# Expert tiles of 96 + 32 slots with one scatter each, and a last token tile routed in halves

## The reference

```
p_g = softmax(h2 @ w_rg + b_rg)                 # 4 groups
g_idx = argmax p_g                              # one group per token
le_sel = logits of the 4 experts of that group
pe_top, e_idx = top_k(softmax(le_sel), 2)       # two experts, both of that group
wts = p_g[g_idx] * pe_top / sum(pe_top)
x = x + sum over the two experts of  wts * (silu(h2 @ w_gate[e]) * (h2 @ w_up[e])) @ w_down[e]
```

## Time and profile before

| | |
|---|---|
| time, median of 3 runs | 559.99 us (556.28 to 560.72) |
| the profiled execution | 559.87 us, span 558.0 us |
| busy in the span | PE 499.4 us (89%), DVE 230.0 (41%), POOL 165.6 (30%), ACT 113.8 (20%) |
| granted TensorE clock, mean | 0.93 |
| scatters that add into `out` (L585) | 25 |

### The profile page before, as it was taken

The page is one execution under the profiler, slowest core; times in us unless marked ns, Lnnn a source line. Parts: engine busy times, 40 slices in busy tenths (PEclk is TensorE's granted clock), DMA queues, the critical chain, the costliest instruction groups (busy, mean ns, idle before and its releaser), DMA issues. The chain is left out here.

```text
span 558.0 us, 7597 instructions
## 1 busy us (share of the span) xinstructions
PE 499.4 (89%) x2858; PEld 267.9 (48%) x2858; DVE 230.0 (41%) x642; ACT 113.8 (20%) x273; POOL 165.6 (30%) x167
## 2 busy tenths in 40 slices
PE   5898899998998999999999997854999999999970
PEld 3554444444664777665666666553333333333320
DVE  1127444412678834444545555452522322223110
ACT  2200242223232243332222311130011000110010
POOL 1211288850789700000000002221035222222242
PEclk9999799998998999999999977665999999999995
DMA  8999500005100000066000229386589999999712
GB/s 290 427 384 404 231 1 1 1 1 194 50 2 0 1 1 0 2 260 267 1 0 1 75 81 374 150 321 234 169 324 342 400 377 388 378 375 380 226 25 32
DMA packets 29609, 100.04 MB, mean 179 GB/s; under 512 B 5376, under 2 KB 6912, under 8 KB 29184
## 3 DMA queue, kind: packets, MB, share of 16 engines
q1 hardware_dynamic: 21216, 84.03, 39.1%
q0 software_dynamic: 5904, 8.43, 6.3%
q10 hardware_dynamic: 2448, 7.04, 3.3%
HBM read 77.39 MB, written 35.21 MB: 202 GB/s over the span
## 5 line engine op out<-in xcount | busy, mean ns | idle before, releaser
L1217 PE MATMUL bank<-arena 128*128 128x512 f32 (+1 forms) x256 | 114.9, 587 | 5.5 <-DVE arena L826 3.1
L1467 PE MATMUL bank<-arena 128*32 128x512 f32 x832 | 93.1, 599 | 0.0
L1192 PE MATMUL bank<-arena 128*128 128x128 f32 (+1 forms) x412 | 61.9, 287 | 21.0 <-DVE arena L908 4.6
L1217 PEld LDWEIGHTS bank<-arena 128*128 128x128 f32 x256 | 49.6, 196 | 61.4 <-issue 54.7
L1192 PEld LDWEIGHTS bank<-arena 128*128 128x128 f32 (+1 forms) x412 | 50.9, 145 | 57.9 <-issue 44.6
L585 POOL DMA_INDIRECT out<-arena x25 | 38.7, 1549 | 122.6 <-DVE arena L1143 49.6
L1355 PE MATMUL bank<-arena 128*128 128x512 f32 x128 | 65.0, 637 | 0.0
L1467 PEld LDWEIGHTS bank<-arena 128*32 128x32 f32 x832 | 25.8, 111 | 57.9 <-issue 57.9
L908 DVE COPY arena<-bank 128x512 f32<-128x512 f32 (+2 forms) x64 | 36.4, 587 | 36.4 <-PE bank L1192 36.3
L467 POOL TENSOR_SCALAR small<-small 128x1 f32<-128x1 f32 x16 | 3.7, 233 | 157.6 <-ACT arena L680 97.1
L1487 PE MATMUL bank<-arena 128*32 128x512 f32 x416 | 47.0, 592 | 0.8 <-DVE arena L1136 0.8
(11 more groups left out here) (153 smaller groups left out, 517.0 us busy)
## 6 DMA issues: line engine op xcount, KB each, us to landing
arena<-in_w_gu SPq DMA_DIRECT2D x17, 2048.0 KB
arena<-in_w_dn SPq DMA_DIRECT2D x17, 1024.0 KB, 20.6
slot_rows<-arena SPq DMA_DIRECT2D x1, 11308.0 KB, 37.8
arena<-slot_rows ACTq DMA_DIRECT2D x13, 514.0 KB, 6.7
arena<-in_w_out SPq DMA_DIRECT2D x2, 2048.0 KB, 8.0
arena<-in_x SPq DMA_DIRECT2D x4, 512.0 KB, 10.7
arena<-in_w_in_k SPq DMA_DIRECT2D x1, 2048.0 KB, 16.3
arena<-in_w_in_q SPq DMA_DIRECT2D x1, 2048.0 KB, 22.3
```

Source lines behind the costliest of these rows:

```text
L1192: last = nc.tensor.transpose(TPB[p % 2][0:s.shape[-1], b * P:(b + 1) * P], s, ident)
L1217: last = nc.tensor.matmul(product_bank(i)[:, 0:width], hT[:, k, t * P:(t + 1) * P], w[:, k, :], start=(k == 0), stop=(k == KD - 1))
L1467: last = nc.tensor.matmul(GU[g % 2][BLK * b:BLK * (b + 1), :], xT[g % 2][:, k, BLK * b:BLK * (b + 1)], w_gu[n % RING][:, k, :], start=(k = ...
```

## The change

It does four things. (1) Tile 3i + j (j = 0, 1, 2) holds the 96 slots of one expert of group i and 32 of the 96 slots of the last expert of group (i + 2) % 4, so no token is in a tile twice. Each tile is added by one scatter, which waits for that of the tile before; 13 scatters take the place of 25. Since own and shared slots lie apart in `slot_rows`, a tile is loaded by two DMAs, of 96 and of 32 rows. (2) Weights are loaded in the order in which tiles need them (`LOADED`), and `buffers()` picks for each load the buffer that is free first. Loads 5 to 16 are issued behind the same tiles as before. (3) `logits_out` finds the two experts by adding -1e30 to the logits of all other groups and taking the top of all 16, in place of cutting out four logits and adding the group's base afterwards. (4) The last token tile is routed in halves: PE and DVE do half b = 0 of its transposes and router products while half b = 1 of the output projection runs; the products of `ranks(3)` with the all-ones matrix are done before the choice is known, in bank 5.

```diff
+TRIPLES = [[EPG * i + j for j in range(3)] + [EPG * ((i + 2) % G) + 3] for i in range(G)]
+LOADED = [TRIPLES[i][j] for i in range(G) for j in (0, 3, 1, 2)]
...
         def loads_of(g):
-            return [(4 * g + b) // 3 if g < ITEMS else E + g - ITEMS for b in range(4)]
+            i, j = divmod(g, 3)
+            return 3 * [4 * i + (0, 2, 3)[j]] + [4 * i + 1] if g < ITEMS else 4 * [E + g - ITEMS]
+        def rows_of(g):
+            if g >= ITEMS:
+                return x_dram[g * P:g * P + CAP, :], x_dram[g * P + CAP:(g + 1) * P, :]
+            i, j = divmod(g, 3)
+            own, shared = CAP * TRIPLES[i][j], CAP * TRIPLES[i][3] + BLK * j
+            return x_dram[own:own + CAP, :], x_dram[shared:shared + BLK, :]
...
-            def add(g, run):
+            def add(g):
                 pool.wait_ge(s_ya, g + 1)
                 pool.wait_ge(s_yv, g + 1)
                 pool.wait_ge(s_tag, g + 1)
+                if g > 0:
+                    pool.wait_ge(s_add[(g - 1) % 3], adds(g - 1))
                 nc.gpsimd.indirect_dma_start(
-                    out=out_rows, out_offset=bass.IndirectOffsetOnAxis(ap=tag_row[:, g, run:run + 1], axis=0),
+                    out=out_rows, out_offset=bass.IndirectOffsetOnAxis(ap=tag_row[:, g, 0:1], axis=0),
...
-                added(g, 0)
-                add(g, 1)
-                add(g + 1, 0)
...
-            added(LAST - 1, 1)
-            add(LAST, 0)
+            for g in range(LAST + 1):
+                add(g)
+                if g < 2:
+                    overflow(2 * g)
+                    overflow(2 * g + 1)
...
-                nc.scalar.dma_start(xg[g % 3], x_dram[g * P:(g + 1) * P, :]).then_inc(s_xg[g % 3], 16)
+                for part, src in ((slice(0, CAP), rows_of(g)[0]), (slice(CAP, P), rows_of(g)[1])):
+                    nc.scalar.dma_start(xg[g % 3][part, :], src).then_inc(s_xg[g % 3], 16)
...
-                link(nc.vector.tensor_scalar(oh, konst[:, K_E:K_E + G], gf, None, ALU.is_equal))
-                link(nc.vector.tensor_tensor(prod.rearrange("p (g e) -> p g e", g=G),
-                                             logits[:, t, :].rearrange("p (g e) -> p g e", g=G),
-                                             oh.unsqueeze(2).to_broadcast([P, G, EPG]), ALU.mult))
-                link(nc.vector.tensor_reduce(ep[:, 0:EPG], prod.rearrange("p (g e) -> p e g", g=G), AX.X, ALU.add))
+                link(nc.vector.tensor_scalar(kept, konst[:, K_GRP:K_GRP + E], gf, NEG, ALU.not_equal, ALU.mult))
+                link(nc.vector.tensor_tensor(kept, kept, logits[:, t, :], ALU.add))
...
-                link(nc.vector.tensor_scalar(gf, gf, float(EPG), None, ALU.mult))
-                link(nc.vector.tensor_scalar(ef, ef, gf, None, ALU.add))
```

More of the change, by code:

```diff
@@ L49, with last_tile, buffers @@
 RING = 5
+TRIPLES = [[EPG * i + j for j in range(3)] + [EPG * ((i + 2) % G) + 3] for i in range(G)]
+LOADED = [TRIPLES[i][j] for i in range(G) for j in (0, 3, 1, 2)]
+def last_tile(n):
+    i, j = divmod(n, 4)
+    return 3 * i + (0, 2, 1, 2)[j] if n < E else ITEMS + n - E
+def buffers():
+    buf, use, before = [], [], []
+    for n in range(E + EXTRA):
+        held = {b: max(m for m in range(n) if buf[m] == b) for b in set(buf)}
+        b = n if n < RING else min(held, key=lambda b: (last_tile(held[b]), held[b]))
+        before.append(held.get(b))
+        buf.append(b)
+        use.append(buf.count(b))
+    return buf, use, before
+BUF, USE, BEFORE = buffers()
 K_TRI, K_ONE, K_E, K_BASE, K_I = 0, P, 2 * P, 2 * P + E, 2 * P + 2 * E
-K_ROW = K_I + EXTRA
-K_CUT = K_ROW + T
-K_MINE = K_CUT + 2 * ITEMS + 1
+K_GRP = K_I + EXTRA
+K_ROW = K_GRP + E
+K_MINE = K_ROW + T
 NK = K_MINE + ITEMS
@@ L308, in loads_of, with adds @@
         def loads_of(g):
-            return [(4 * g + b) // 3 if g < ITEMS else E + g - ITEMS for b in range(4)]
[L312 to L317, removed]
+            i, j = divmod(g, 3)
[6 more added lines that the diff above has]
+            return x_dram[own:own + CAP, :], x_dram[shared:shared + BLK, :]
+        def adds(g):
+            return 16 * (g // 3 + 1)
         def passes(eng, extra):
@@ L1427, in _ @@
             router(2)
-            for b in range(2):
-                for part in range(2):
-                    out_projection(("b", T - 1, b), part)
+            for part in range(2):
+                out_projection(("b", T - 1, 0), part)
+            out_projection(("b", T - 1, 1), 0)
             ranks(2)
             side_turn(("h2", T - 1, 0))
+            out_projection(("b", T - 1, 1), 1)
+            for i in range(T - 1):
+                nc.tensor.matmul(KB_OF[T - 1][:, 32:32 + E], konst[:, K_ONE:K_ONE + P], sels[:, i, 0:E],
+                                 start=(i == 0), stop=False)
+            router(T - 1, (0,))
             side_turn(("h2", T - 1, 1))
-            router(T - 1)
-            ranks(T - 1)
+            router(T - 1, (1,))
+            pe.wait_ge(s_sel, T)
+            nc.tensor.matmul(KB_OF[T - 1][:, 32:32 + E], konst[:, K_TRI:K_TRI + P], sels[:, T - 1, 0:E],
+                             start=False, stop=True).then_inc(s_rank, 1)
             for t in range(T):
@@ L1553 @@
     p = np.arange(P, dtype=f32)
[L1554 removed]
     konst = np.concatenate([
         np.triu(np.ones((P, P), f32), 1), np.ones((P, P), f32), np.tile(p[:E], (P, 1)),
[L1557 to L1559 removed]
+        np.tile(CAP * p[:E], (P, 1)), np.tile(p[:EXTRA], (P, 1)), np.tile(p[:E] // EPG, (P, 1)), p[:, None] + P * p[:T] - FAR,
+        *[np.where(p < CAP, t[j], t[3])[:, None] for t in TRIPLES for j in range(3)]], axis=1).astype(f32)
     def by_expert(v, blocks):
```

128 lines of the change are left out of this document (54 added, 74 removed).

## The result

The changed kernel takes 567.37 us (median of 4 runs, 562.19 to 568.02) against 558.13 us for the kernel before (4 runs, 553.20 to 560.72): a ratio of 1.0177, interval 1.0121 to 1.0233. It is slower, where 554.2 us and a range of 551.0 to 557.0 had been forecast. The ratios in this text compare the fast runs of both kernels and are not the quotients of the two medians (that would be 1.0166 here). Its profiled span is 566.3 us, 8.3 us more than the 558.0 before.

What follows compares the result with a forecast made beforehand. Between about 386 and 542 us PE was taken to bound the kernel, with DMA engines just as full. From 559.87 us, -5.5 (tail), -0.3 (up to the tile load) and +0.15 (split load) gave 554.2 us, range 551.0 to 557.0.

Steps and rivals of the forecast that it cites:

- The split load: Tile loads as two DMAs: first tile's second part issued later, loads otherwise limited by bytes; +0.15 us, from 0 to 0.45.
- PE still without a wait in the tiles: Sign expected in the profile after: PE has no waits in the expert tiles.
- Rival (c): First tile load: its two parts serialize, +3.4 us, 557.4 us; sign, PE waits over 4 us before transposes; chance 0.06.
- Rival (d): Expert tiles: full scatters land slower than 10.5 us, their chain sets the end from 12.0; 569.9 us at 13; chance 0.04.
- The loop: scatters in a chain: Expert tiles: one chained scatter per tile needs 11.3 us, under PE's 11.67, so it costs 0.
- The tail: one scatter per tile: After the last tiles: the last scatter starts earlier with one scatter per tile; -5.5 us, between 4.65 and 6.47 gained.
- rival (b): Tail saves only 3.0 to 3.7 us, by a short step or tile 11's longer scatter; 556.0 to 556.7 us; chance 0.11.
- The choice on DVE: Expert choice, token tile 1: 0.65 us less on DVE, part perhaps lost to PE's lower clock; -0.33 us taken.
- The last token tile: Routing in halves ahead of the expert tiles: 3.4 us saved, `dispatch(3)` issued at about 374.4 in place of 377.75.
- What is late next: DMA traffic of stores and weights, full till about 379, delays `dispatch(3)`; only -0.3 us up to the tile load.

Runs made afterwards that it cites:

- the early stores: Stores of x of the first three token tiles issued before the wait for the last output projection: 0.9865 on the changed kernel with one load per tile, 1.0003 on the kernel before.
- the kernel with one load: Changed kernel with slots laid out tile by tile in DRAM, so each tile is one DMA of 128 rows: 552.02 us, 0.9938 of the kernel before.
- grouped form: Kernel before with tiles loaded by 96 + 32 rows, the DRAM side written as groups of eight rows: 562.78 us, 1.0159.

## Why the prediction was wrong

**"The split load"** is the step that failed: "The loads are limited by bytes once they run", +0.15 us. The split alone costs 1.0216 on the kernel before, and taking it out of the changed kernel goes from 1.0177 to 0.9938, 2.4%. I priced it by the issue at the first tile. What it costs is bandwidth for all later tiles, the weights' with it. The bounds (0 to 0.45) were made from an issue time, which says nothing of that; no row of before shows a load of fewer rows, so an honest upper end had to come from asking what a few per cent of bandwidth would cost. That much could be asked: the engines were full at 1.02, the reserve was only what PE had not yet needed, and the 34 GB/s that were missing over 40 us are 1.4 MB, more than half the gate and up weights of one expert. "PE still without a wait in the tiles" was the sign to look for, and it failed.

**Rival (c)** had the right edit and the wrong place. Its sign came true, since PE waited 386.10 - 381.71 = 4.4 us from that load to its transposes, over the 4 named, but its price didn't: that is 1.0 more than before, not 3.4, and nothing in the loop was in it. It also means that +0.15, with 0.45 as its most, was too small at the first tile itself. The Trainium skill ("DMA: Bandwidth & Descriptors", section "Rules for kernel authors") advises one transfer over 128 partitions, and the runs agree with the advice. That its reason, that the two serialize, makes the loss they don't show: at the first tile it could explain 1.0 us at most, and the row parts slow the weights as well, which are no part of the two.

**Rival (d)**, the slow case, also fell. Scatters landed in 5.9 to 11.1 us (median 9.5), under the 12.0 from which the chain would decide; POOL waited for DVE's results in 11 of 13 cases. The time came out near its 569.9 by another mechanism.

**"The loop: scatters in a chain"**, 0, held as far as the scatters go.

**"The tail: one scatter per tile"**, -5.5: measured from the last DVE result to the end of the span, 566.3 - (554.96 + 0.75) = 10.6 us against 558.0 - 542.67 = 15.3, so -4.7, next to the smallest gain that I allowed (4.65). The mechanism was right and the landing mis-sized: tile 11's scatter took 6.0 us where I had 5.0, so the step was 558.56 - 551.69 = 6.87 in place of the 5.8 that stands behind -5.5, and the last scatter started 2.85 us behind the last DVE result and not 1.6. Two sums beside this term were turned round. A shorter step can't make the gain smaller, since the end before is measured: with a step of 3.4 the last scatter would have waited for its own result only, a gain of 6.47 and not 3.7. So of rival (b) only the longer scatter was a way to a smaller gain.

**"The choice on DVE"**: PE's wait for `logits_out(1)` went from 3.68 to 3.04 us, -0.64; forecast -0.65. That only half of it comes through, because PE would be back at the upper clock no sooner, these traces can't tell: the 16 products of the last output projection took 7.36 + 1.88 = 9.2 us in place of 8.6, but 9.3 to 9.5 in three traces of kernels with the old routing (the splits by 96 + 32 rows and by columns, and the early stores on the kernel before).

**"The last token tile"** and **"What is late next"**: `dispatch(3)` was issued at 373.01, 4.7 earlier, where I had 374.4 and -3.4. Of the 4.7, 1.4 were there at `ranks(1)` already (345.94 against 347.32), 0.6 of them from the choice on DVE and the rest chance; the last token tile gave 3.4. The dispatch landed in 7.5 us and not 3.5, inside the 6 to 8 I named, and the transposes came at 386.10 against 385.80: the gain was swallowed as forecast, 0.3 late and not 0.3 early, and 1.7 late by the distance from `ranks(1)`, of which the split load is 1.0. The stretches say by what:

```profile
374.00:378.00 4.00, 0.00 (x0) 0.00 (x0) 0.00 (x0) 0.00 (x0) 0.97 (x1) 0.50 1.02 416
378.00:380.00 2.00, 0.00 (x0) 0.00 (x0) 0.00 (x0) 0.00 (x0) 0.00 (x0) 0.50 1.04 417
380.00:382.00 2.00, 0.00 (x0) 0.00 (x0) 0.00 (x0) 0.00 (x0) 0.00 (x0) 0.50 0.39 156
```

The engines are full until 380 and not 378. The early stores show the cause by taking it away: in both kernels that have the shorter chain and the early stores the dispatch lands in 3.2 us.

Without the split the sum would have been close: 559.87 - 4.7 and nothing at the head is 555.2, and the kernel with one load took 552.02 (0.9938 of its own runs of before, which is 556.4 by the 559.87 that I started from).

## What to carry to other kernels

An engine without waits beside DMA engines that are full has no reserve that the profile shows: price an edit of any DMA there by the bandwidth of all, not by its own issue or bytes. All four splits by rows cost here and the split by columns did not: load whole 128-row tiles, and if rows of two sources must meet, lay them out together in DRAM when they are written. When a chain is shortened and the time doesn't move, look at what traffic the earlier step now falls into; a store that can go earlier may be what is missing. And compare two traces from a point just ahead of the edit: here what lay ahead differed by up to 8 us between executions.

## What the runs showed of the hardware

Loads of the same bytes in row groups of 96 + 32, 64 + 64, 112 + 16 and 120 + 8 made this kernel 1.9 to 3.0% slower (96 + 32 in its grouped form 1.6%), two column halves 0.2%, which is no difference. With the row groups the DMA engines stayed full (shares 1.00 to 1.03) and moved 315 to 333 GB/s from 400 to 440 us in place of 352.

Why is open. It isn't the number of DMAs (column halves), nor the uneven size (64 + 64), nor the weights' order; and the second small DMA accounts for a part at most (8 rows beside a whole load, 0.5%, with 0 in the interval; 32 rows 1.0%). I had thought it was that both parts use all 16 engines with fewer rows each, and so with other rows. The Trainium skill ("DMA: Bandwidth & Descriptors", section "Why a DMA increments its semaphore by 16 and not by 1") gives a DMA the largest number of engines up to 16 that divides its rows, which is 15 and 8 for 120 + 8 rows, 8 rows to an engine as in a whole load. The packets agree: 2539 are 7 more for each of 13 tiles than 2448, and 15 + 8 is 7 more than 16. Yet this was the slowest by its median, so 8 rows to an engine are not enough. Which eight rows each engine took no run shows, so that it matters which engine writes which rows is not shut out; it stays a theory.

A scatter that adds took 4.7 us to land when it held one expert's rows of a tile and 6.0 when it held a whole tile's, with little traffic beside it in either case; in the loop it took up to 11.1. By the GB/s of the stretches these were some 0.16 and 0.31 MB, an estimate. The dispatch of 1.05 MB landed in 3.2 to 3.5 us on free engines and in 7.5 beside the stores and the weights.
